# A two-layer decoder trunk on one core: a block's rows are scaled before they are turned, and the next projection's first four tiles start before the last turn

## What is computed

```python
h = rms_norm(x, norm_g[layer, 0]) * (1.0 + sc_m) + sh_m
y = gdn_mixer(h, ...)            # layer 1: dsa_mixer(h, ...)
x = x + (1.0 + ga_m) * rms_norm(y, norm_g[layer, 1])
h = rms_norm(x, norm_g[layer, 2]) * (1.0 + sc_f) + sh_f
y = swiglu(h, ffn_w_in[layer], ffn_w_out[layer])
x = x + (1.0 + ga_f) * rms_norm(y, norm_g[layer, 3])
```

## Time and profile before

| what | us |
|---|---|
| median of 3 runs | 1426.42 (1426.35 to 1429.85) |
| the profiled execution, whole | 1427.37 |
| its span | 1425.8 |
| PE busy | 1358.3 (95%) |
| DVE busy | 806.5 (57%) |
| ACT busy | 568.8 (40%) |
| POOL busy | 124.3 (9%) |

### The profile page before, as it was taken

One profiled execution on the slowest core, in us unless ns is written; L12 is line 12 of the kernel. 1 busy time (PEld: TensorE's weight loads), 2 busy tenths in 40 slices (PEclk: granted clock), 3 DMA queues, 4 the chain that ended last, 5 costly groups with the idle time before them and its releaser, 6 DMA issues.

```text
span 1425.8 us, 18300 instructions
## 1 busy us (share of the span) xinstructions
PE 1358.3 (95%) x7087; PEld 1096.8 (77%) x7087; DVE 806.5 (57%) x1392; ACT 568.8 (40%) x1079; POOL 124.3 (9%) x142
## 2 busy tenths in 40 slices
PE   3799999989999999999999999999999999999998
PEld 3678887888888877887888865655888888888886
DVE  4877867457465655555556659776453333233335
ACT  3366865455342212221233655586352212222231
POOL 0002020016100000000000002030000000000000
PEclk9899999999999999999999999999999999999999
DMA  9555322112235455555532210010122222321321
GB/s 325 183 178 177 119 89 90 33 58 88 90 102 194 177 177 177 177 177 178 177 118 89 69 44 30 30 42 20 60 83 94 88 89 90 117 89 59 118 89 59
DMA packets 102855, 158.39 MB, mean 111 GB/s; under 512 B 9325, under 2 KB 74106, under 8 KB 102778
## 3 DMA queue, kind: packets, MB, share of 16 engines
q1 hardware_dynamic: 91898, 115.40, 24.6%
q0 software_dynamic: 10880, 41.95, 8.6%
HBM read 155.24 MB, written 2.10 MB: 110 GB/s over the span
## 4 chain that ended last, share of the span: by engine, by line
PE 84%; DVE 7%; ACT 5%; issue 2%; DMA 1%; SPq 0%; POOL 0%; DVEq 0%; POOLq 0%; ACTq 0%
PE ps L400 14%; PE ps L402 14%; PE ps L401 14%; PE ps L2044 4%; PE ps L2046 4%; PE ps L2045 4%; PE ps L750 3%; PE ps L752 3%; PE ps L751 3%; PE ps L728 2%; PE ps L2416 1%; PE ps L515 1%; DVE w_lo L384 1%; PE ps L2183 1%; PE ps L2441 1%
## 5 line engine op out<-in xcount | busy, mean ns | idle before, releaser
L400 PE MATMUL ps<-h_hi,w_hi 128*128 128x512 f32 x912 | 364.2, 399 | 0.0
L402 PE MATMUL ps<-h_hi,w_lo 128*128 128x512 f32 x912 | 360.6, 395 | 0.0
L401 PE MATMUL ps<-h_lo,w_hi 128*128 128x512 f32 x912 | 360.5, 395 | 0.0
L384 DVE TENSOR_TENSOR w_lo<-raw,w_hi 128x1024 fp32r<-128x1024 f32 x172 | 209.1, 1221 | 240.9 <-ACT w_hi L378 240.4
L378 ACT ACTIVATE w_hi<-raw 128x1024 fp32r<-128x1024 f32 x180 | 188.2, 1050 | 147.0 <-PE ps L2046 142.8
L402 PEld LDWEIGHTS ps<-h_hi,w_lo 128*128 128x128 f32 x912 | 172.1, 189 | 40.5
L400 PEld LDWEIGHTS ps<-h_hi,w_hi 128*128 128x128 f32 x912 | 172.4, 189 | 39.4 <-issue 0.5
L401 PEld LDWEIGHTS ps<-h_lo,w_hi 128*128 128x128 f32 x912 | 172.2, 189 | 39.5 <-issue 0.5
L496 DVE SCALAR_TENSOR_TENSOR ada_acc<-ada_in,c_act,ada_acc 128x512 f32<-128x512 f32 x154 | 115.6, 751 | 4.1
L1908 ACT ACTIVATE g_hi<-tmp 128x512 fp32r<-128x512 f32 x44 | 27.8, 632 | 210.9 <-DVE tmp L1943 210.9
L2044 PE MATMUL ps<-w_hi,g_hi 128*128 128x512 f32 x256 | 101.6, 397 | 2.6 <-DVE w_lo L384 2.6
(11 more groups left out here) (390 smaller groups left out, 2074.8 us busy)
## 6 DMA issues: line engine op xcount, KB each, us to landing
raw<-in_ffn_w_in_dram SPq DMA_DIRECT2D x44, 1024.0 KB, 5.1
ada_in<-in_ada_w_dram POOLq DMA_DIRECT2D x40, 1024.0 KB, 5.6
raw<-in_ffn_w_out_dram SPq DMA_DIRECT2D x20, 1024.0 KB, 5.1
raw<-in_gdn_w_in_dram SPq DMA_DIRECT2D x16, 1024.0 KB, 5.9
ada_in<-in_ada_w_dram SPq DMA_DIRECT2D x4, 1024.0 KB, 9.3
x_t<-in_x_dram SPq DMA_DIRECT2D x2, 2048.0 KB, 9.8
early_slab<-in_ada_w_dram SPq DMA_DIRECT2D x4, 1024.0 KB, 14.1
raw<-in_gdn_w_out_dram SPq DMA_DIRECT2D x4, 1024.0 KB, 4.9
```

What stands on the lines that cost most here:

```text
L384: ops.tensor_tensor(lo, raw_tile(s, kc) if src is None else src, f32(hi), ALU.subtract).then_inc(lo_done, 1)
L400: nc.tensor.matmul(out_, hi[:, k, :], r_hi[:, k, :], start=k == 0, stop=False)
L401: nc.tensor.matmul(out_, hi[:, k, :], r_lo[:, k, :], start=False, stop=False)
L402: last = nc.tensor.matmul(out_, lo[:, k, :], r_hi[:, k, :], start=False, stop=k == kc - 1)
```

## The change

The scaling by the inverse root no longer sits in the matmul. A scaled copy `XS` of a block's rows is made, its first half by DVE (where `diag` was made), its second half by ACT, and PE only transposes it against the identity. ACT's half stands in its list behind the squares of x, ahead of `nxt(0)` and `nxt(1)`. In the last block DVE, not ACT, rounds weight tiles 2 and 3 (`high_beside`): tile 2 between the scaling of y and the variance (for even `m` between the two halves of the scaling), tile 3 ahead of the variance of x. `pe_first_tokens` runs tiles 0, 1, 2 ahead of the last turn and tile 3 behind it (`m` = 0), all four ahead (`m` = 1), or tiles 0, 1, 2 (`m` = 2, whose tile 3 stays whole). `pe_last_tokens` does the rest of each. The broadcast of the gate goes to banks 4 and 5.

```diff
-        def pe_first_tokens(pe, q):
+        def pe_first_tokens(pe, q, m, tiles):
             part = slice(0, 2 * P)
-            for s in range(2):
+            for s in tiles:
                 pe.wait_ge(hi_done, q * 4 + s + 1)
+                if s >= 2 and m % 2:
+                    pe.wait_ge(sem("y_added"), 8 * (m // 2) + 2 * (NB - 1) + s - 1)
+                elif s >= 2:
+                    pe.wait_ge(sem("row_sq"), sq_no(m, NB - 1, 0) + s - 1)
+                    pe.wait_ge(sem("y_scaled"), 8 * m + 2 * (NB - 1) + s - 1)
...
+        FIRST_TILES = [((0, 1, 2), (3,)), ((0, 1, 2, 3), ()), ((0, 1, 2), ())]
+
-        def pe_last_tokens(pe, q, m):
+        def pe_last_tokens(pe, q, m, tiles):
...
+        xs_at = cb_at - 4096
+        XS = [fixed(f"xs{m}", [P, D], at=conv_u_at if m == 0 else xs_at) for m in range(3)]
...
         def pe_turn_x(pe, m, b):
-            pe.wait_ge(sem("x_diag"), diag_no(m, b))
             if b >= 2:
                 pe.wait_ge(sem("h_made"), 8 * OUT_H[m] + 2 * (b - 2) + 2)
             for g in range(2):
+                pe.wait_ge(*((sem("x_diag"), diag_no(m, b)) if g == 0 else (sem("x_normed"), NB * m + b + 1)))
                 for d in range(4):
-                    last = nc.tensor.matmul(ps[:, 4 + 2 * (b % 2) + g, d * P:(d + 1) * P],
-                                            x_t[:, b, (4 * g + d) * P:(4 * g + d + 1) * P], diag[:, b, :],
-                                            start=True, stop=True)
+                    last = nc.tensor.transpose(ps[:, 4 + 2 * (b % 2) + g, d * P:(d + 1) * P],
+                                               XS[m][:, (4 * g + d) * P:(4 * g + d + 1) * P], ident[:, :])
...
             if m < 3:
-                pe_first_tokens(pe, (Q_FFN[0], Q_DSA, Q_FFN[1])[m])
+                pe_first_tokens(pe, NEXT_Q[m], m, FIRST_TILES[m][0])
                 pe_turn_x(pe, m, NB - 1)
+                pe_first_tokens(pe, NEXT_Q[m], m, FIRST_TILES[m][1])
             if 1 <= m < 3:
-                pe_cb(pe, m + 1, 2)
+                pe.wait_ge(sem("h_affine"), DC + 12 * m + 12)
+                pe.wait_ge(sem("h_scaled"), DC + 20 * m + 12)
+                pe_cb(pe, m + 1, 4)
...
+                act.wait_ge(sem("row_root"), row(m, b, 1) + 2)
+                nc.scalar.activation(XS[m][:, S:D], x_t[:, b, S:D], ACT.Copy, scale=row_rinv[:, 1, b:b + 1])\
+                    .then_inc(sem("x_normed"), 1)
                 if b == 2:
                     nxt(0)
                     nxt(1)
             if m < 3:
                 h_last(NB - 1)
                 if m:
-                    act_cb(act, m + 1, 2)
-                nxt(2)
-                nxt(3)
+                    act_cb(act, m + 1, 4)
...
+            def high_beside(s):
+                q = NEXT_Q[m]
+                dve.wait_ge(raw_in[s // 2], q * 16 + 16)
+                dve.wait_ge(tile_done, 4 * (q - 2) + s + 1)
+                dve.wait_ge(hi_done, 4 * q + s)
+                nc.vector.tensor_copy(split_tile(w_hi, s), raw_tile(s)).then_inc(hi_done, 1)
...
+                    if m < 3 and b == NB - 1 and j == m % 2:
+                        high_beside(2)
...
             def root(b):
+                if b == NB - 1:
+                    high_beside(3)
...
-                nc.vector.tensor_scalar(diag[:, b, :], ident[:, :], row_rinv[:, 1, b:b + 1], None, ALU.mult)\
+                nc.vector.tensor_scalar(XS[m][:, 0:S], x_t[:, b, 0:S], row_rinv[:, 1, b:b + 1], None, ALU.mult)\
                     .then_inc(sem("x_diag"), 1)
...
-                        if start and s < 2:
-                            if s == 0:
-                                pe_last_tokens(pe, q, 2 * layer)
+                        if start and (s < 3 or layer == 0):
+                            if s != 1:
+                                pe_last_tokens(pe, q, 2 * layer, ((0, 1), (), (2,), (3,))[s])
...
                 if s == 0:
-                    pe_last_tokens(pe, Q_DSA, 1)
+                    pe_last_tokens(pe, Q_DSA, 1, (0, 1))
                 elif s >= 2:
-                    pe_tile(pe, Q_DSA, s, h_hi, h_lo)
+                    pe_last_tokens(pe, Q_DSA, 1, (s,))
```

More of the change, by code:

```diff
@@ L216, in build_trunk @@
         q_eps = gdn("q_eps", [P, NB, H])
+        conv_u_at = gdn.at
         conv_u = [gdn(f"conv_u{i}", [P, S + 8]) for i in range(2)]
@@ L713, in turn_no @@
             return DC + 1 + 9 * m + 2 * b + g + 1
+        xs_at = cb_at - 4096
+        XS = [fixed(f"xs{m}", [P, D], at=conv_u_at if m == 0 else xs_at) for m in range(3)]
+        NEXT_Q = (Q_FFN[0], Q_DSA, Q_FFN[1])
         Y_MM = [0, 20, 28, 48]
```

## The result

The changed kernel took 1413.2 us (median of 4 runs, 1411.83 to 1415.19) beside 1427.7 (median of 4, 1426.35 to 1429.85) for the kernel before, a ratio of 0.9901 with a 95% interval of 0.9889 to 0.9912: 14.5 us faster. The profiled execution has a span of 1410.3 where that of before had 1425.8. The forecast was 1411, which is 15.5 less than before.

A forecast was written before the change was run, and what follows sets the result against it. PE, busy 95% of the span, was taken as the bound. Passage savings of 6.2, 4.8 and 4.5 us sum to 15.5, giving 1411.9 from the profiled 1427.37 or 1410.9 from the median 1426.42; 1411 taken, range 1408 to 1416.

The forecast's parts named there:

- The turn, 0.88 for 1.79: PE's turn behind each block: 8 transposes at 0.109 replace 8 fp32 matmuls at 0.224, saving 0.91 us a turn.
- third rival: A transpose takes a quarter of the matmul's 0.224, 0.056; the kernel would take 1406.5 us; chance 0.04.
- Nine turns as pure PE time, 8.2: Turns behind blocks 1, 2 and 3 in three passages save 8.2 us of PE time if their input is there.
- slack of 0.3: Behind block 2 of passage 1, ACT's half is ready at 8.9 and the next turn asked for at 9.2.
- Scaled rows: 0.49 on DVE, 0.63 on ACT: Last block's scaled rows: started at T'+5.99, done at 6.48 on DVE and 6.62 on ACT; PE waits for nothing.
- The copies at 0.75, hidden: DVE's copies of tiles 2 and 3 take 0.75 us each in idle stretches; at 1.22, 1.7 us lost in all.
- `w_lo` 1 at T'+12.0: Passage 0: DVE's list behind the scaled rows ends at 12.0, PE needs it at 11.96: no hole, no slack.
- first rival: The turns save, the filling doesn't: DVE lacks slack, collisions cost another 1 us a passage; 1415.5 us, chance 0.11.
- The passages 6.2, 4.8, 4.5: Savings in us in passages 0, 1 and 2, from shorter turns and filled idle time and holes.
- Nothing here hands the gain back.: Behind each passage PE is the bound; the next quad's tiles come well ahead of T'+24.5, so the gain stays.
- The sum, 15.5, and 1411: Whole kernel: the three passages' savings sum to 15.5 us, giving 1411.9 or 1410.9, taken as 1411.
- The clock as the slower rival, 0.02: Fourth rival: PE's clock falls from 2.4 to 1.2 GHz behind each turn, costing 22 us: 1433; chance 0.02.

The follow-up runs named there:

- turns_twice: The changed kernel with the transposes of blocks 0, 1 and 2 each issued twice; 1423.92 us, 10.7 slower than the changed kernel.
- dve_extra: The changed kernel with one more 128x512 DVE copy behind the last block's scaled rows in each passage; 1418.19 us, ratio 0.9925.
- turns_only: The kernel before with only the scaled copy `XS` and its transposes, weight tiles as before; 1426.56 us, ratio 0.9989.
- fill_only: The changed kernel with the matmul by the diagonal matrix kept, DVE still rounding tiles 2 and 3 early; 1423.61 us, ratio 0.9966.
- lo_early: The changed kernel with `w_lo` of tile 1 made between the two groups of `h_scale` in the last block; 1412.94 us, ratio 0.99.
- lo_again: lo_early once more, unchanged, on the same chip as a later kernel; 1412.36 us, ratio 0.9889.
- turns_hot: turns_only with useless matmuls ahead of each passage's last turn, 14 in passages 0 and 2, 28 in passage 1; 1424.18 us, ratio 0.9977.
- both: lo_early with the first FFN's small matmuls on the modulation slab's sum moved behind a quad's second weight tile; 1412.92 us, ratio 0.9901.
- after_again: The changed kernel once more, unchanged, on the same chip as lo_early and both; 1413.18 us, ratio 0.9904.

## Why the prediction was right

- *The turn, 0.88 for 1.79.* 0.87. The distances of two other groups of transposes held here. The factor of four for fp32 that the Trainium skill gives ("TensorE: Matmul & The Clock Gate", table of terms) did not: the third rival is out.
- *Nine turns as pure PE time, 8.2.* Right. In passage 1 ACT's half of block 2 was there 9.07 behind block 2's end (786.10 - 777.03) and the turn was due at 9.21, so the slack of 0.3 was 0.1. turns_twice gives the price from the other side, 0.87 for each.
- *Scaled rows: 0.49 on DVE, 0.63 on ACT.* 0.49 and 0.72. ACT's half was sized by a plain copy; the excess of 0.09 delayed nothing.
- *The copies at 0.75, hidden.* 0.68, and hidden, with 0.34 us to spare. Taking the one-input form's slope was right; at the upper bound of 1.22 they would have lain on the chain.
- *`w_lo` 1 at T'+12.0.* 406.60 + 1.22 - 395.87 = 11.95, in passage 2 1040.92 + 1.22 - 1030.19 = 11.95. This counts from the record of the turn; from the chain's piece (396.03), as the prediction counts, it is 11.79. dve_extra shows that there is no slack behind it, as the first rival said. That rival's further microsecond a passage did not come.
- *The passages 6.2, 4.8, 4.5.* 6.22, 4.66, 4.63. In passage 1 the block's chain did come 0.8 later on ACT, and the four tiles did cover it. From block 2's turn to the second quad it took 24.57 in passage 0, 26.35 in passage 2 and, less the statistics matmuls, 26.4 in passage 1; 24.5, 26.4 and 26.3 had been forecast.
- *"Nothing here hands the gain back."* Wrong by 0.86: the slab's sum in FFN 0. I looked at whether the next quad's tiles came in time and not at the other work that DVE does behind the same DMA. The load moved from 16.1 to 12.4 ahead of the second quad.
- *The sum, 15.5, and 1411.* The passages gave 15.5, which is the forecast met by its mechanism. 0.86 went in FFN 0, and 0.58 in the rest for a reason that isn't shown. That leaves 14.1 to 14.6 for the edit, and the medians say 14.5. The span's 15.5 holds 1.4 that the code ahead of the passages gave by chance. Against the later median of before, 1427.7, the same sum would have given 1412.2.
- *The clock as the slower rival, 0.02.* In the changed kernel the clock stayed at 1.00 in all three passages. But the argument was too easy. I set idle time beside it as something that the change takes away, and did not ask what each part does alone: turns_only lost the clock at the last turn of every passage. And I misread the attention's rows: of the 78 matmuls between 915 and 925 us 22 are transposes (line 2441), not half. The stretch speaks less against that rival than I made of it; turns_twice, with 16 transposes in a row at 1.00, speaks more.

Where the expected gain came from: the transposes with the clock held up are worth 6.3, the filling alone 5.3, both 15.5. So with the filling in place the twelve turns bring 10.2 of their 11.0. A shorter turn at the end of a passage is mostly idle time until there is work to put there. And the work alone gains little: in passage 0 of fill_only the last turn starts 7.49 behind block 2's turn, where it started 6.82 behind it before and 6.67 in the changed kernel. There the third tile, 1.90, fills the idle 1.08 and delays the last turn.

## What to carry to other kernels

A shortening in front of a wait on a chain over other engines is worth little by itself: work out what PE will do while it waits, and make that part of the same change. When a part of a change measures at nothing, look at the granted clock around the gaps before calling its mechanism wrong; filling the gap with useless matmuls is a cheap test. For a copy moved to another engine, find the idle stretch by who ended it and how long it was, and then ask what stands behind the next DMA that the moved instruction lets go.

## What the runs showed of the hardware

- The clock's fall costs what the earlier trace rows price it at: 0.43 for 0.23. One fall in the attention stage made that stage 1.1 to 1.2 longer (lo_early, lo_again, turns_only).
- It isn't fixed by the code of the stage: the same wait of 2.6 us for `cq_lo` had a fall in it or behind it in turns_only, turns_hot, fill_only, turns_twice, dve_extra, lo_early, lo_again and both, and none in the kernel before, the changed kernel and after_again. The attention of dve_extra was 2.85 us longer with two falls in it, though no instruction there was changed. Whether the edit brought them or chance did isn't shown: the changed kernel and after_again are one code, and so are lo_early and lo_again; each pair agrees, but a pair is two profiled executions.
- The statement of the Trainium skill ("TensorE: Matmul & The Clock Gate", Part 4) that transposes don't count as busy for the clock as matmuls do was not tested by itself: the falls in turns_only stand behind idle time and transposes together. The changed kernel's turns of 0.87 among matmuls, and those of turns_twice at 1.75, left the clock at 1.00.
- A copy of 1024 fp32 columns from SBUF to fp32r on DVE took 0.68 us (ACT 1.05), and of 512 fp32 columns to fp32 0.42 (dve_extra).
